# The order of products inside the feed-forward units whose weights are the stationary operand

## The chip, the cores and the metric

The kernel runs on one core of a Trainium2 chip. The metric is the device time of one execution in microseconds (us); lower is better. All inputs and the output are float32, with a batch of one and 256 positions.

## The reference, cut to what matters

Two transformer blocks follow one another. The parts that the change touches are their two feed-forward layers:

```
# first block: D_MODEL = 1024, D_FF = 4096
u = rms_norm(h, g_mlp)
h = h + jnp.square(jax.nn.relu(u @ w_ff1)) @ w_ff2
...
# second block: D_FF_2 = 2816
h2 = _rmsnorm(x, norm2_w) * (1.0 + scale2) + shift2
ffn = jnp.dot(jax.nn.silu(jnp.dot(h2, w_ffn_gate)) * jnp.dot(h2, w_ffn_up), w_ffn_down)
x = x + gate2 * ffn
```

## The kernel before, in words

Every weight matrix is read once, in units of 128 partitions by two contraction tiles by 512 columns (`raw`). ScalarE rounds a unit to its upper half (`w_hi`), VectorE subtracts to get its lower half (`w_lo`), both in a ring of four slots (`SPLIT`). The activations are kept the same way, upper and lower half side by side (`xT`, `sT`: contraction tile, half, 256 positions). A product in full precision is the sum of three: upper by upper, lower by upper, upper by lower.

Two kinds of unit matter here.

- In most units the activations are the stationary operand and 512 columns of weights move past them: `unit_pair`, `unit_rows` and `unit_wide`, all through `mm3` (L1709 to L1711), three products of 512 columns into one bank.
- In the feed-forward layers the hidden units are wanted transposed, so the weights are the stationary operand. `unit_T2` does this. A unit has four column tiles (i = 0 to 3), and each has its own PSUM bank `B[:, i, :]`. For each tile, two products of 512 columns (L1772, one for each contraction tile kk: `w_hi` by both halves of the activations side by side) and then two of 256 columns (L1775: `w_lo` by the upper half, added to the second half of the same bank). That makes 16 products a unit.

Four such units make the hidden units of a chunk, and are followed by `unit_wide` units, which multiply the previous chunk's hidden units with the second matrix: four of them in the first block (`hidden_chunk`, called for seven chunks), two in the second (`two_chunks`, ten chunks). Only these two functions call `unit_T2`.

What orders the work around it: before a unit, TensorE waits for `lo_done` (the unit's lower half is there). In the first unit of a chunk it also waits ahead of tile 0 and ahead of tile 2 for a count of `relu` or `ffn_sums`: the earlier content of banks 0 and 1, then of banks 2 and 3, has been read out. In the last unit, the last product of tile 1 adds to `first_bank`, upon which ScalarE copies from banks 0 and 1 (`hidden_minor` L743, `ffn_minor`, its copy at L962); the last product of every unit adds to `units_used`, upon which ScalarE may fill the slot anew (L787 in the first block's loop, L982 in the second's).

`unit_T2_banks` (L1787, L1790; the first block's input projection) and the 256-column products of `unit_T` (L1757 to L1759) are like it in kind and aren't changed. `unit_pair_lows_last` (L1734, L1743, L1746) takes two units near the start of the kernel: 512-column products whose bank alternates from each product to the next.

Of the kernel before, what the change touches and what calls it, by code (L numbers as in the profile page):

```python
# [7 lines left out]
P = 128  # L8
# [7 lines left out]
SEQ = 256  # L16
# [155 lines left out]
def build(nc, x, p, g_mix, w_in, b_forget, swa_sinks, w_br_swa, w_br_fox, w_mix_out, g_mlp, w_ff1, w_ff2,  # L172
# [87 lines left out]
    with ExitStack() as ctx:  # L260
        def sb(name, shape, dt=F32):
            return ctx.enter_context(nc.sbuf_tensor(name, shape, dt))
# [3 lines left out]
        def sem(name):  # L266
            return sems[name]
# [3 lines left out]
        w_hi = sb("w_hi", [P, SPLIT, 2, 512], F32R)  # L271
        w_lo = sb("w_lo", [P, SPLIT, 2, 512], F32R)
# [127 lines left out]
        B = ctx.enter_context(nc.psum_tensor("B", [P, 8, 512], F32))  # L400
# [1305 lines left out]
        def _(pe):  # L1706
            def mm3(bank, xh, xl, wh, wl, start, stop):

                nc.tensor.matmul(bank, xh, wh, start=start, stop=False)  # L1709
                nc.tensor.matmul(bank, xh, wl, start=False, stop=False)  # L1710
                return nc.tensor.matmul(bank, xl, wh, start=False, stop=stop)  # L1711
# [12 lines left out]
            def rows_of(t):  # L1724

                return slice(t * P, (t + 1) * P)
# [37 lines left out]
            def unit_T2(u, x2, kt0, first, last, sums=None, free=None):  # L1764

                s = u % SPLIT
                for i in range(4):
                    if free is not None and i % 2 == 0:
                        pe.wait_ge(sem(sums), free + i // 2)
                    cols = slice(i * P, (i + 1) * P)  # L1770
                    for kk in range(2):
                        nc.tensor.matmul(B[:, i, :], w_hi[:, s, kk, cols], x2[:, kt0 + kk, :, :].rearrange("p e n -> p (e n)"),  # L1772
                                         start=first and kk == 0, stop=False)
                    for kk in range(2):
                        m = nc.tensor.matmul(B[:, i, SEQ:2 * SEQ], w_lo[:, s, kk, cols], x2[:, kt0 + kk, 0, :], start=False,  # L1775
                                             stop=last and kk == 1)
                    if last and i == 1:
                        m.then_inc(sem("first_bank"), 1)
                m.then_inc(units_used, 1)

# [13 lines left out]
            def unit_rows(u, xh, xl, kt0, t, bank, first, last):  # L1794

                s, n = u % SPLIT, spans(u)
                rows = slice(t * P, (t + 1) * P)
                for kk in range(2):
                    m = mm3(B[:, bank, 0:n], xh[:, kt0 + kk, rows], xl[:, kt0 + kk, rows], w_hi[:, s, kk, 0:n], w_lo[:, s, kk, 0:n],
                            first and kk == 0, last and kk == 1)  # L1800
                return m
# [99 lines left out]
            for c in range(5):  # L1901
                banks = (2 * (c % 2), 2 * (c % 2) + 1)
                for kp in range(4):
# [12 lines left out]
                    if u == 1:  # L1916
                        for kk, (upper_half, lower_half) in enumerate(((sem("second_hi"), sem("second_lo")), (hi_done, lo_done))):
# [8 lines left out]
                            for t in range(TILES):  # L1926
                                m = nc.tensor.matmul(B[:, banks[t], :], xT_hi[:, 2 + kk, rows_of(t)], w_lo[:, 1, kk, :], start=False, stop=False)
# [9 lines left out]
                    else:  # L1937
                        for kk, (x_upper, upper_half, x_lower, lower_half) in enumerate((
# [9 lines left out]
                            for t in range(TILES):  # L1948
                                m = nc.tensor.matmul(B[:, banks[t], :], xT_hi[:, kk, rows_of(t)], w_lo[:, 0, kk, :], start=False, stop=False)
# [7 lines left out]
                    if u == 6:  # L1957

                        pe.wait_ge(sem("root_id"), 2)
                        for t in range(TILES):  # L1960
                            m = nc.tensor.matmul(B[:, 6, t * P:(t + 1) * P], ones, rstd_id[:, t, :], start=True, stop=True)
# [13 lines left out]
            for n in range(2 * HEADS + 4):  # L1975
# [10 lines left out]
                else:  # L1986
                    i = n - 16
# [78 lines left out]
            def hidden_chunk(j, opens):  # L2066

                for r in range(4):
                    pe.wait_ge(lo_done, j * 8 + (U_FFL + r - 7))
                    unit_T2(U_FFL + r, sT, 2 * r, r == 0, r == 3, "relu", j * 2 - 1 if r == 0 else None)  # L2070
                for r in range(4):
                    if r % 2 == 0:
                        pe.wait_ge(sem("hid_lo"), j * 2 - (1 if r == 0 else 0))
                    pe.wait_ge(lo_done, j * 8 + (U_FFL + r - 3))
                    unit_wide(U_FFL + 4 + r, xT_hi, xT_lo, r, acc, opens and r == 0, False)
# [35 lines left out]
            for kp in range(4):  # L2111
                pe.wait_ge(lo_done, U_PG + 4 + kp + 1)
                m = unit_rows(U_PG + 4 + kp, sT_hi, sT_lo, 2 * kp, 0, 6, kp == 0, kp == 3)
# [34 lines left out]
            for q in range(4, 60):  # L2148
# [20 lines left out]
                if 13 <= q < 21 and (q - 13) % 2 == 0:  # L2169
                    i = q - 13  # L2170
# [6 lines left out]
                if 33 <= q < 41 and (q - 33) % 2 == 0:  # L2177
                    n = q - 17
# [13 lines left out]
                if q >= 44 and (q - 44) % 3 == 0 and (q - 44) // 3 < R_HEADS:  # L2192
                    i = (q - 44) // 3
# [7 lines left out]
                if q >= 46 and (q - 46) % 3 == 0 and (q - 46) // 3 < R_HEADS:  # L2201
                    i = (q - 46) // 3
# [40 lines left out]
            for t in range(TILES):  # L2243
                for i, (half, kp) in enumerate(SQUARE[4:8], 4):
# [9 lines left out]
                    m = unit_rows(u, sT_hi, sT_lo, 2 * kp, t, 4 + 2 * half + t, False, kp == 3)  # L2254
# [22 lines left out]
            def two_chunks(i, opens, last=False):  # L2277

                for half in range(2):
                    for e in range(6):  # L2280
                        u = U_FNL + 6 * half + e
                        if e == 4:
                            pe.wait_ge(sem("ffn_lo"), i * 2 + (half + 1))
                        pe.wait_ge(lo_done, i * 12 + (u + 1))
                        if e < 4:
                            unit_T2(u, xT, 2 * e, e == 0, e == 3, "ffn_sums", i * 4 + (2 * half + 1) if e == 0 else None)
                        else:
                            unit_wide(u, sT_hi, sT_lo, 2 * half + e - 4, acc, opens and half == 0 and e == 4, False,
                                      7 if last and half and e == 5 else None)
# [8 lines left out]
            for t in range(TILES):  # L2298
                rows = slice(t * P, (t + 1) * P)
                for half in range(2):  # L2300
                    own = t == 1 and half == 1
                    for piece in range(2 if own else 1):
                        n = SEQ if own else 2 * SEQ
                        cols = slice(SEQ * piece, SEQ * piece + n)
                        for e in range(2):
                            k = (U_FNE + e) % SPLIT
                            o = B[:, piece if own else acc[t][half], 0:n]
                            if t == 0 and half == 0 and e == 1:
# [4 lines left out]
                                m = nc.tensor.matmul(o, sT_hi[:, e, rows], w_lo[:, k, half, cols], start=False, stop=True)  # L2313
                                continue
                            m = mm3(o, sT_hi[:, e, rows], sT_lo[:, e, rows], w_hi[:, k, half, cols],
                                    w_lo[:, k, half, cols], own and e == 0, e == 1)
# [28 lines left out]
```

## Time and profile before

| what | value |
|---|---|
| median of 3 runs | 824.3 us (824.13 to 824.35) |
| the profiled execution's own time | 823.81 us |
| its span, first to last instruction | 822.1 us |
| mean granted TensorE clock | 0.998 |
| TensorE matmul busy | 812.8 us (99%) |
| weight loads busy | 677.7 us (82%) |
| VectorE, ScalarE, GpSimd busy | 629.3, 462.9, 61.9 us |

Matmuls are pipelined and the end of one in the trace is modelled, so the duration of a product overlaps the next one's. What a product costs is read from the distance of its start to the next product's start. In the timeline, products of one line that follow each other are merged into one row with their count. "PEld" is the weight load ahead of each product; each of the products has its own.

### The profile page before, as it was taken

The page shows a single profiled execution, that of the slowest core. Times are in us where ns is not written, and L with a number is a line of the kernel's source. Part 1 is how long each engine was busy: PE and PEld are TensorE (multiplying, and loading weights), DVE is VectorE, ACT ScalarE, POOL GpSimd, SP SyncE. Part 2 cuts the span into 40 slices and gives each one's busy share as a digit, 9 for nine tenths or more (in the row PEclk, how much of TensorE's full clock was granted, in tenths as well). Part 3 has the DMA queues.
Part 4 walks back from the last instruction along what each step waited for, and adds up shares of the span by engine and source line. Part 5 has one row for each costly group of instructions (what it writes and reads, how often), then busy time and mean ns, then how long its engine had stood idle before and what let it go on. Part 6 is the DMA issues. An engine that isn't in the chain of part 4 may idle for free.

```text
span 822.1 us, 12294 instructions
## 1 busy us (share of the span) xinstructions
PE 812.8 (99%) x4272; PEld 677.7 (82%) x4272; DVE 629.3 (77%) x965; ACT 462.9 (56%) x751; POOL 61.9 (8%) x89
## 2 busy tenths in 40 slices
PE   9999999999999999999999999999999999999996
PEld 7897777898888888877978877888888888888885
DVE  5567777687888898878878997456796877677776
ACT  6657765466555555568544466446346654455444
POOL 2100000110011110301510000010000000000000
PEclk9999999999999999999999999999999999999999
DMA  9867435779999999543965574555544666655641
GB/s 302 275 198 237 136 126 182 251 273 405 346 335 340 319 323 336 191 120 106 272 213 143 164 218 137 171 154 153 180 154 128 201 189 209 196 178 172 209 130 52
DMA packets 89213, 173.15 MB, mean 211 GB/s; under 512 B 6553, under 2 KB 37001, under 8 KB 89041
## 3 DMA queue, kind: packets, MB, share of 16 engines
q1 hardware_dynamic: 83008, 142.56, 54.2%
q0 software_dynamic: 6000, 29.93, 10.5%
q8 instruction: 27, 0.44, 0.2%
q14 instruction: 18, 0.14, 0.0%
q10 hardware_dynamic: 160, 0.07, 0.0%
HBM read 170.42 MB, written 1.06 MB: 209 GB/s over the span
## 4 chain that ended last, share of the span: by engine, by line
PE 95%; DVE 2%; issue 1%; ACT 1%; POOLq 0%; POOL 0%; ACTq 0%; DVEq 0%
PE B L1709 19%; PE B L1711 19%; PE B L1710 19%; PE B L1772 15%; PE B L1775 8%; PE B L1852 2%; PE B L1787 2%; PE B L1882 2%; PE B L1860 1%; PE B L1873 1%; PE B L2126 1%; PE B L1790 1%; DVE w_lo L1032 1%; PE B L1818 0%; PE B L1809 0%
## 5 line engine op out<-in xcount | busy, mean ns | idle before, releaser
L1032 DVE TENSOR_TENSOR w_lo<-raw,w_hi 128x1024 fp32r<-128x1024 f32 (+3 forms) x154 | 184.8, 1209 | 49.4 <-ACT w_hi L569 47.9
L1709 PE MATMUL B<-w_hi,xT 128*128 128x512 f32 (+3 forms) x536 | 209.5, 391 | 0.0
L569 ACT ACTIVATE w_hi<-raw 128x1024 fp32r<-128x1024 f32 (+3 forms) x154 | 157.5, 1030 | 88.6 <-PE B L1711 74.6
L1711 PE MATMUL B<-w_hi,xT 128*128 128x512 f32 (+3 forms) x536 | 204.5, 381 | 0.0
L1710 PE MATMUL B<-w_lo,xT 128*128 128x512 f32 (+3 forms) x536 | 204.1, 381 | 0.0
L1709 PEld LDWEIGHTS B<-w_hi,xT 128*128 128x128 f32 x536 | 100.8, 188 | 20.7 <-issue 2.2
L1711 PEld LDWEIGHTS B<-w_hi,xT 128*128 128x128 f32 x536 | 100.7, 188 | 19.8
L1710 PEld LDWEIGHTS B<-w_lo,xT 128*128 128x128 f32 x536 | 100.9, 188 | 17.4
L1772 PE MATMUL B<-xT,w_hi 128*128 128x512 f32 x320 | 100.5, 395 | 0.0
L982 ACT ACTIVATE w_hi<-raw 128x1024 fp32r<-128x1024 f32 x60 | 62.2, 1055 | 42.5 <-PE B L1775 30.9
L1302 DVE TENSOR_TENSOR w_lo<-raw,w_hi 128x1024 fp32r<-128x1024 f32 x56 | 67.2, 1221 | 21.7 <-ACT w_hi L787 20.8
L1709 PE MATMUL B<-w_hi,sT 128*128 128x512 f32 (+1 forms) x201 | 78.9, 393 | 0.0
L1638 DVE TENSOR_TENSOR w_lo<-raw,w_hi 128x1024 fp32r<-128x1024 f32 x60 | 72.5, 1220 | 7.6 <-ACT w_hi L982 7.6
L1710 PE MATMUL B<-w_lo,sT 128*128 128x512 f32 (+1 forms) x201 | 77.9, 388 | 0.0
L1711 PE MATMUL B<-w_hi,sT 128*128 128x512 f32 (+1 forms) x201 | 77.9, 387 | 0.0
L787 ACT ACTIVATE w_hi<-raw 128x1024 fp32r<-128x1024 f32 x56 | 57.5, 1053 | 35.0 <-PE B L1775 30.6
L1775 PEld LDWEIGHTS B<-xT,w_lo 128*128 128x128 f32 x320 | 60.1, 188 | 14.1
L1772 PE MATMUL B<-sT,w_hi 128*128 128x512 f32 x224 | 70.3, 395 | 0.0
L1775 PE MATMUL B<-xT,w_lo 128*128 128x256 f32 x320 | 62.9, 278 | 0.0
L1310 DVE SCALAR_TENSOR_TENSOR Z<-Z,small 128x1536 f32<-128x1536 f32 x28 | 50.8, 1813 | 0.0
L1775 PEld LDWEIGHTS B<-sT,w_lo 128*128 128x128 f32 x224 | 42.1, 188 | 9.9
L1772 PEld LDWEIGHTS B<-xT,w_hi 128*128 128x128 f32 x320 | 49.4, 189 | 0.9 <-DVE Z L1624 0.2
(270 smaller groups left out, 1071.4 us busy)
## 6 DMA issues: line engine op xcount, KB each, us to landing
raw<-in_w_in_dram SPq DMA_DIRECT2D x79, 512.0 KB, 3.9
raw<-in_w_ff_dram SPq DMA_DIRECT2D x64, 512.0 KB, 7.4
Z<-in_w_ada_dram POOLq DMA_DIRECT2D x32, 768.0 KB, 7.6
raw<-in_w_ffn_gate_dram SPq DMA_DIRECT2D x44, 256.0 KB, 3.4
raw<-in_w_ffn_up_dram SPq DMA_DIRECT2D x44, 256.0 KB, 4.1
raw<-in_w_ffn_down_dram SPq DMA_DIRECT2D x20, 512.0 KB, 4.3
raw<-in_w_mix_out_dram SPq DMA_DIRECT2D x8, 512.0 KB, 3.7
raw<-in_w_ple_gate_dram SPq DMA_DIRECT2D x8, 512.0 KB, 4.3
```

Of the source, the lines that this page charges most:

```text
L569: nc.scalar.activation(w_hi[:, u % SPLIT, :, 0:n], raw[:, st.slot[u], :, 0:n], ACT.Copy).then_inc(hi_done, 1)
L787: nc.scalar.activation(w_hi[:, u % SPLIT, :, :], raw[:, st.slot[u], :, :], ACT.Copy).then_inc(hi_done, 1)
L982: nc.scalar.activation(w_hi[:, u % SPLIT, :, :], raw[:, st.slot[u], :, :], ACT.Copy).then_inc(hi_done, 1)
L1032: nc.vector.tensor_tensor(w_lo[:, u % SPLIT, :, 0:n], raw[:, st.slot[u], :, 0:n], w_hi[:, u % SPLIT, :, 0:n].bitcast(F32), ALU.subtract).t ...
L1302: nc.vector.tensor_tensor(w_lo[:, u % SPLIT, :, :], raw[:, st.slot[u], :, :], w_hi[:, u % SPLIT, :, :].bitcast(F32), ALU.subtract).then_in ...
L1310: nc.vector.scalar_tensor_tensor(ada_acc[:, 1536 * q:1536 * (q + 1)], ada_raw[:, q, :], silu_now, ada_acc[:, 1536 * q:1536 * (q + 1)], ALU ...
L1638: nc.vector.tensor_tensor(w_lo[:, u % SPLIT, :, :], raw[:, st.slot[u], :, :], w_hi[:, u % SPLIT, :, :].bitcast(F32), ALU.subtract).then_in ...
L1709: nc.tensor.matmul(bank, xh, wh, start=start, stop=False)
L1710: nc.tensor.matmul(bank, xh, wl, start=False, stop=False)
L1711: return nc.tensor.matmul(bank, xl, wh, start=False, stop=stop)
L1772: nc.tensor.matmul(B[:, i, :], w_hi[:, s, kk, cols], x2[:, kt0 + kk, :, :].rearrange("p e n -> p (e n)"), start=first and kk == 0, stop=False)
L1775: m = nc.tensor.matmul(B[:, i, SEQ:2 * SEQ], w_lo[:, s, kk, cols], x2[:, kt0 + kk, 0, :], start=False, stop=last and kk == 1)
```

## The change

In `unit_T2` the column tiles are taken in pairs (b = 0: tiles 0 and 1, b = 1: tiles 2 and 3). For a pair, the four 512-column products come first: contraction tile 0 for both tiles, then contraction tile 1 for both; so the bank alternates from product to product, and two products in a row have the same moving operand. Then come the pair's four 256-column products in the same order. The products themselves, their number, the waits ahead of tiles 0 and 2 and the increments behind tile 1 and behind the unit are those of before.

```diff
             def unit_T2(u, x2, kt0, first, last, sums=None, free=None):
 
                 s = u % SPLIT
-                for i in range(4):
-                    if free is not None and i % 2 == 0:
-                        pe.wait_ge(sem(sums), free + i // 2)
-                    cols = slice(i * P, (i + 1) * P)
+                for b in range(2):
+                    if free is not None:
+                        pe.wait_ge(sem(sums), free + b)
                     for kk in range(2):
-                        nc.tensor.matmul(B[:, i, :], w_hi[:, s, kk, cols], x2[:, kt0 + kk, :, :].rearrange("p e n -> p (e n)"),
-                                         start=first and kk == 0, stop=False)
+                        for i in (2 * b, 2 * b + 1):
+                            nc.tensor.matmul(B[:, i, :], w_hi[:, s, kk, i * P:(i + 1) * P], x2[:, kt0 + kk, :, :].rearrange("p e n -> p (e n)"),
+                                             start=first and kk == 0, stop=False)
                     for kk in range(2):
-                        m = nc.tensor.matmul(B[:, i, SEQ:2 * SEQ], w_lo[:, s, kk, cols], x2[:, kt0 + kk, 0, :], start=False,
-                                             stop=last and kk == 1)
-                    if last and i == 1:
+                        for i in (2 * b, 2 * b + 1):
+                            m = nc.tensor.matmul(B[:, i, SEQ:2 * SEQ], w_lo[:, s, kk, i * P:(i + 1) * P], x2[:, kt0 + kk, 0, :], start=False,
+                                                 stop=last and kk == 1)
+                    if last and b == 0:
                         m.then_inc(sem("first_bank"), 1)
                 m.then_inc(units_used, 1)
```

## Rows read from the trace of the kernel before

**Rows 1.** The page: the span, the engines' busy time, the chain by engine.

```profile
span 822.1 us, 12294 instructions
...
PE 812.8 (99%) x4272; PEld 677.7 (82%) x4272; DVE 629.3 (77%) x965; ACT 462.9 (56%) x751; POOL 61.9 (8%) x89
...
PE 95%; DVE 2%; issue 1%; ACT 1%; POOLq 0%; POOL 0%; ACTq 0%; DVEq 0%
```

**Rows 2.** Waits of TensorE, longest in total (the only row).

```profile
PE B L1890 <- DVE ones_r L1130: 1.4, 1, 1.4
```

**Rows 3.** Groups by line and shape on TensorE: unit_T2's products.

```profile
L1772 PE MATMUL B<-xT,w_hi 128*128 128x512 f32 x320 | 100.5, 395 | 0.0
...
L1772 PE MATMUL B<-sT,w_hi 128*128 128x512 f32 x224 | 70.3, 395 | 0.0
L1775 PE MATMUL B<-xT,w_lo 128*128 128x256 f32 x320 | 62.9, 278 | 0.0
L1775 PE MATMUL B<-sT,w_lo 128*128 128x256 f32 x224 | 44.0, 278 | 0.0
```

**Rows 4.** Line L1775: who waited for it (us in total, times).

```profile
  ACT Z L962: 35.9, 19
  ACT w_hi L982: 30.9, 18
```

**Rows 5.** Timeline of TensorE in a unit_T2 stretch: start, duration in us.

```profile
303.19 0.63 PE L1772 MATMUL B<-sT,w_hi 128*128 128x512 f32 x2
303.65 0.39 PE L1775 MATMUL B<-sT,w_lo 128*128 128x256 f32 x2
303.88 0.62 PE L1772 MATMUL B<-sT,w_hi 128*128 128x512 f32 x2
304.35 0.40 PE L1775 MATMUL B<-sT,w_lo 128*128 128x256 f32 x2
304.58 0.63 PE L1772 MATMUL B<-sT,w_hi 128*128 128x512 f32 x2
```

**Rows 6.** Timeline: the first product of one unit_T2 stretch, and the first behind it.

```profile
316.17 0.39 PE L1772 MATMUL B<-sT,w_hi 128*128 128x512 f32 x1
...
327.30 0.40 PE L1709 MATMUL B<-w_hi,xT 128*128 128x512 f32 x1
```

**Rows 7.** Timeline of the second unit in unit_pair_lows_last.

```profile
16.24 1.07 PE L1734 MATMUL B<-w_hi,xT 128*128 128x512 f32 x4
17.15 1.07 PE L1746 MATMUL B<-w_lo,xT 128*128 128x512 f32 x4
18.05 1.07 PE L1743 MATMUL B<-w_hi,xT 128*128 128x512 f32 x4
```

**Rows 8.** Timeline where 256-column products (unit_T) follow products of 512 columns.

```profile
171.61 0.28 PE L1757 MATMUL B<-sT,w_hi 128*128 128x256 f32 x1
171.72 0.28 PE L1758 MATMUL B<-sT,w_hi 128*128 128x256 f32 x1
...
172.08 0.28 PE L1758 MATMUL B<-sT,w_hi 128*128 128x256 f32 x1
...
172.68 0.28 PE L1757 MATMUL B<-sT,w_hi 128*128 128x256 f32 x1
```

**Rows 9.** Timeline where products of 512 columns follow a run of 256-column ones.

```profile
399.50 0.40 PE L1709 MATMUL B<-w_hi,xT 128*128 128x512 f32 x1
...
400.43 0.39 PE L1710 MATMUL B<-w_lo,xT 128*128 128x512 f32 x1
400.66 0.39 PE L1711 MATMUL B<-w_hi,xT 128*128 128x512 f32 x1
400.89 0.39 PE L1709 MATMUL B<-w_hi,xT 128*128 128x512 f32 x1
```

**Rows 10.** Windows: busy time by engine, then PEclk, the granted clock.

```profile
15.90:18.80 2.90, 2.90 (x15) 2.39 (x14) 2.06 (x4) 2.87 (x7) 0.00 (x0) 1.00 1.10 352
...
316.10:327.40 11.30, 11.30 (x67) 9.85 (x66) 10.79 (x11) 5.38 (x6) 0.53 (x1) 1.00 0.95 318
```

**Rows 11.** Timeline of TensorE's first products of the kernel.

```profile
1.44 2.93 PE L1890 MATMUL B<-ones_r 128*128 128x512 f32 x6 [1.44 <-DVE ones_r L1130]
...
5.37 1.20 PE L1890 MATMUL B<-ones_r 128*128 128x512 f32 x2
```

## The prediction

> **What bounds the kernel now.** I read the page first. TensorE is busy 99% of the span and holds 95% of the chain that ended last [rows 1]; the other engines are well below. Then its waits: in the whole span TensorE waits once for another engine, 1.4 us at the very start [rows 2]. So the kernel lasts as long as its 4272 products take one behind another, and an edit that moves nothing but the order of products can only work through their spacing. The groups by line say how many are touched: 320 + 224 of 512 columns at L1772 and as many of 256 columns at L1775 [rows 3], 1088 in all, or 68 units, or 136 pairs of column tiles. The durations there (395 and 278 ns) overlap and are no price. The price is in the timeline: two column tiles, 303.19 to 304.58, take 1.39 us [rows 5]. A whole stretch of four units, eight pairs, takes 327.30 - 316.17 = 11.13 us [rows 6], 1.391 us for a pair, and the stretches that I compared are alike. All 136 pairs are 189 us, 23% of the span.
>
> **What the change removes and adds: nothing but an order.** A pair has four products of 512 columns and four of 256 before and after, each with its own weight load. The waits for the banks stand ahead of the first and the ninth product of a unit in both versions. `first_bank` comes with the eighth product and `units_used` with the sixteenth in both. That matters because ScalarE is queued behind these two: it waits 35.9 us in all for the copies at L962 and 30.9 us for the slots at L982 [rows 4]. Since the counts of products ahead of each signal are the same, ScalarE, VectorE behind it, and the DMAs that refill the raw slots see each signal earlier or later only by what the pairs themselves gain or lose; I cost them at nothing. Their cover is that TensorE doesn't wait on them now [rows 2]; with a pair some ns longer they have more room. Were pairs shorter, the most they could be late is the gain itself.
>
> **The price of four 512-column products in a row.** Within the present pattern the two starting at 303.19 take 0.46 us and the two at 303.88 take 0.47 us, so about 0.233 us each [rows 5]. Two other places give bounds. (a) `unit_pair_lows_last` is the nearest form: runs of four, the bank alternating with each product, the same moving operand twice in succession, as after the change. Its first two runs of four take 17.15 - 16.24 = 0.91 and 18.05 - 17.15 = 0.90 us, 0.227 a product [rows 7]. But these are in the middle of an all-512 stretch. So neither an alternating bank nor a repeated moving operand costs or saves anything by itself. (b) Behind a run of 256-column products, the first four of 512 columns take 400.43 - 399.50 = 0.93 us, and only then does a product come to 0.23 and less [rows 9]. After the change, every run of four follows 256-column products, so (b) is the nearer case. I take 0.93, with 0.91 and 0.94 (four times 0.235, a little over the present pattern) as ends.
>
> **The price of four 256-column products in a row.** In the present pattern two take 0.23 us: 303.88 - 303.65 and 304.58 - 304.35 [rows 5], about 0.116 each. In `unit_T`, the first one behind products of 512 columns takes 0.11 us, and the first four 172.08 - 171.61 = 0.47 us; the nine shown take 172.68 - 171.61 = 1.07 us, so a later one costs 0.12 [rows 8]. The short price of 0.11 is thus had only directly behind the long products; today each pair of tiles gets it twice, after the change once. I take 0.47, with 0.46 (four at today's 0.116) and 0.48 (four at 0.12) as ends.
>
> **The sum.** A pair after the change: 0.93 + 0.47 = 1.40 us, against 1.391, so +0.009 us. Times 136 pairs: +1.2 us. The rows are rounded to 0.01 us, and 0.01 us a pair is 1.4 us, so the sign is weak. Order inside the `unit_wide` behind each of 17 stretches might shift by some 0.01 us, 0.2 us in all, which I leave out. Against the profiled execution that is 823.81 + 1.2 = 825.0; it stands 0.5 us below the median of the runs, so against the median the forecast is 824.3 + 1.2 = 825.5 us, +0.15%.
>
> A measurement of this kernel can tell about 0.2%, 1.65 us, from no change; that is 0.012 us a pair.
>
> **A rule of the Trainium skill beside it.** Rows say that the spacing of one kind of product depends on what stands ahead of it (0.93 against 0.91 us for four of 512 columns, 0.11 against 0.12 for one of 256) [rows 7, 8, 9]. The Trainium skill, page "TensorE: Matmul & The Clock Gate", section "Back-to-back issue gap", gives the isolated gap at the high clock as the columns over 2.4 plus 2.5 ns, that is 216 and 109 ns, and a lower figure for streams with weight loads, 131 ns at 512 columns. The trace doesn't agree with either: 227 and 120 ns in long runs. By that rule order doesn't enter and the change would be worth exactly nothing: 824.3 us.
>
> **The rivals.**
>
> *The short switches go, and nothing else (0.20).* Long runs stand at 0.227 and 0.12 us a product. If the present pattern's surplus over these is a cost of each switch between 512 and 256 columns, the pair loses half its switches: 4 x 0.2267 + 4 x 0.12 = 1.387 us is the floor, 4 ns below 1.391; with half the surplus left 1.389. That is -0.3 to -0.6 us: 823.9 us, no measurable change. For it: 512-column products do settle at 0.227 [rows 7]. Against it: they need more than four products to settle behind short ones [rows 9].
>
> *Faster (0.06).* The four long products settle at once (0.907, as in rows 7) and the four short ones keep the price of rows 8 (0.47): 1.377 us, -0.014 a pair, -1.9 us: 822.4 us. It counts as faster only if both hold. Against it: the short 0.11 looks like a lead that is given back in the next long products, whose first four take 0.93; both at once would take the lead and not return it.
>
> *Slower: every run stays unsettled (0.12).* Four of 512 columns at 0.235 and four of 256 at 0.12, as if the weight load ahead of each short product set its pace: 0.94 + 0.48 = 1.42 us, +0.029 a pair, +3.9 us: 828.2 us. It decides from +0.012 a pair on. For it: runs of 256 columns stand at 0.12 [rows 8] although two in a row have 0.116 now, and the first product behind a run of short ones is as long as 0.235. Against it: by the fourth long product the spacing has fallen to 0.23 [rows 9].
>
> *The granted clock falls (0.02).* Granted clock is 1.00 in the present stretches and also where banks alternate with each product [rows 10], and TensorE has no gap that the new order would open. Products of 512 columns did stand 2.93 / 6 = 0.49 us apart at the kernel's start, 2.15 times as far [rows 11]; if one stretch of 11.13 us ran so, it would cost 12.8 us: 837 us. The Trainium skill, same page, section "A second HAM failure mode: psum-queue depth-cycling", tells of a kernel with 512-column products that cycled through banks each iteration, idled briefly between groups and so had its clock swing; that speaks against this change, and the alternating unit at 16.24 us does not show it.
>
> **How the numbers follow.** The forecast has 0.60, with its own range 1.395 to 1.405 us a pair, +0.5 to +1.9 us: 824.8 to 826.2 us. A little of it, 0.04, lies above the 0.2% bound. Within 0.2%: 0.56 + 0.20 = 0.76. Slower: 0.04 + 0.12 + 0.02 = 0.18. Faster: 0.06. For 8 in 10 the range takes the forecast and the settled case and stops short of the outer two: from 823.5 (the floor of 1.387, less a little for the runs' spread) to 827.0 us (1.411 a pair, between the forecast's end and the unsettled case).
>
> **What the changed profile would show.** The timeline's merged rows hold four products each, L1772 and L1775 in turn. Right: such a period lasts 1.40 us, a stretch of four units 11.2 us, the four long ones 0.93 and the four short ones 0.47; PEclk stays 1.00; the waits of TensorE stay at one row; the ScalarE waits behind the last short product are as long as before within a few us. The settled rival shows 11.10 to 11.12 us a stretch, the faster one 11.02, the unsettled one 11.36. What would make the prediction wrong: a spacing inside runs of four that no place in this trace has, above all of 256-column products that alternate between two banks, the one form that it doesn't show; or new rows in TensorE's waits at the bank waits.

## The result, and the profile after

The changed kernel takes 825.45 us (median of 22 runs, 825.11 to 827.31), the kernel before 824.12 us in 22 runs of the same comparison; the ratio is 1.0018, 95% interval 1.0012 to 1.0024. That is 1.3 us by the medians and 1.5 us by the ratio: a real but very small loss. The ratio lies just inside the 0.2% that the prediction set as its bound; the upper end of the interval, 0.24%, lies outside it. The forecast was 825.5 us.

The page of the changed kernel: span, busy time, chain by engine [against rows 1].

```profile
span 823.5 us, 12294 instructions
...
PE 814.2 (99%) x4272; PEld 679.1 (82%) x4272; DVE 629.4 (76%) x965; ACT 462.8 (56%) x751; POOL 61.8 (8%) x89
...
PE 98%; issue 0%; DVE 0%; ACT 0%; POOLq 0%; POOL 0%; ACTq 0%; DVEq 0%
```

The same 4272 products, and 1.4 us more of TensorE busy for 1.4 us more of span; VectorE, ScalarE and GpSimd have the busy times that they had, within 0.1 us. TensorE's waits, whole list [against rows 2]:

```profile
PE B L1891 <- DVE ones_r L1130: 1.4, 1, 1.4
PE B L1944 <- ACT w_hi L643: 0.2, 1, 0.2
```

The second wait is one at the kernel's start, in code that the change doesn't touch; some of the experiments below have it and some don't. No wait has come in the feed-forward layers. But the list leaves one out in both kernels. The first stretch of the second block is longer than the others, 11.453 against 11.137 us before and 11.500 against 11.200 after, because TensorE stands ahead of tile 2 until VectorE has read out the banks. The products' modelled ends cover this gap; the rows of the weight loads show it, before and after:

```profile
644.27 0.30 PEld L1772 LDWEIGHTS B<-xT,w_hi 128*128 128x128 f32 x2 [0.22 <-DVE Z L1624]
...
644.80 0.30 PEld L1772 LDWEIGHTS B<-xT,w_hi 128*128 128x128 f32 x2 [0.22 <-DVE Z L1624]
```

So the prediction's "TensorE waits once" [rows 2] is one wait short, and this wait matters in the runs of eight and sixteen below. It is as long after the change as before. So the loss is in the spacing of products. Timeline of TensorE: start, duration, count, at the end of one stretch of `unit_T2`, and the first products behind it [against rows 5, 9].

```profile
302.91 1.09 PE L1772 MATMUL B<-sT,w_hi 128*128 128x512 f32 x4
303.84 0.64 PE L1776 MATMUL B<-sT,w_lo 128*128 128x256 f32 x4
304.31 1.09 PE L1772 MATMUL B<-sT,w_hi 128*128 128x512 f32 x4
305.24 0.63 PE L1776 MATMUL B<-sT,w_lo 128*128 128x256 f32 x4
305.71 0.40 PE L1709 MATMUL B<-w_hi,xT 128*128 128x512 f32 x1
...
316.64 0.61 PE L1772 MATMUL B<-sT,w_hi 128*128 128x512 f32 x2
...
327.84 0.40 PE L1709 MATMUL B<-w_hi,xT 128*128 128x512 f32 x1
```

Four products of 512 columns take 303.84 - 302.91 = 0.93 us and four of 256 take 304.31 - 303.84 = 0.47 us; the pair 1.40. In single starts, a pair in the middle of a stretch has 932 ns for its long products and 461 for its short ones before, and 929 and 474 after (the mean of a unit's two pairs): the loss is in the short ones. The whole stretch takes 327.84 - 316.64 = 11.20 us against 11.13 [rows 6]. Windows of the changed kernel, with the granted clock behind POOL's column [against rows 10]:

```profile
316.10:327.40 11.30, 11.30 (x65) 9.79 (x64) 10.69 (x11) 5.37 (x6) 0.74 (x2) 1.00 0.90 314
```

The clock stays at 1.00.

The starts in the trace, taken to the nanosecond, make the account of the span's 1.4 us (1.47 unrounded). All 17 stretches of `unit_T2` sum to 190.73 us against 189.65, +1.08. The `unit_wide` units behind fifteen of them (those followed by another stretch) sum to 114.90 against 114.43, +0.48: a run of 48 products took 305.71 to 316.64 = 10.93 us above, and 10.89 before, as these rows of the kernel before show.

```profile
305.28 0.40 PE L1709 MATMUL B<-w_hi,xT 128*128 128x512 f32 x1
...
316.17 0.39 PE L1772 MATMUL B<-sT,w_hi 128*128 128x512 f32 x1
```

The units behind the first stretch of each block took the same as before; those behind each of the other thirteen took 0.037 us more. The units behind the two stretches left out of the fifteen add 0.07 us. Everything else is 0.16 us shorter, 0.1 of it ahead of the first stretch; two executions of one kernel differ by more.

### The profile page after: what moved, and what is told of

It reads as the page before. It is cut to its first block, busy times and chain, and to the rows that moved or that the text cites. A ratio compares the mean times of both kernels' runs of the same rounds, so it can differ in the third digit from the quotient of the medians.

```text
span 823.5 us, 12294 instructions
## 1 busy us (share of the span) xinstructions
PE 814.2 (99%) x4272; PEld 679.1 (82%) x4272; DVE 629.4 (76%) x965; ACT 462.8 (56%) x751; POOL 61.8 (8%) x89
## 4 chain that ended last, share of the span: by engine, by line
PE 98%; issue 0%; DVE 0%; ACT 0%; POOLq 0%; POOL 0%; ACTq 0%; DVEq 0%
PE B L1709 20%; PE B L1711 20%; PE B L1710 20%; PE B L1772 15%; PE B L1776 8%; PE B L1853 2%; PE B L1788 2%; PE B L1883 2%; PE B L1861 1%; PE B L1874 1%; PE B L2127 1%; PE B L1791 1%; PE B L1819 0%; PE B L1810 0%; PE B L1821 0%; PE B L1759 0%
## 5 line engine op out<-in xcount | busy, mean ns | idle before, releaser
L1772 PE MATMUL B<-xT,w_hi 128*128 128x512 f32 x320 | 87.2, 394 | 0.0
L982 ACT ACTIVATE w_hi<-raw 128x1024 fp32r<-128x1024 f32 x60 | 62.2, 1054 | 43.1 <-PE B L1776 31.1
L787 ACT ACTIVATE w_hi<-raw 128x1024 fp32r<-128x1024 f32 x56 | 57.5, 1053 | 35.7 <-PE B L1776 30.9
L1772 PEld LDWEIGHTS B<-xT,w_hi 128*128 128x128 f32 x320 | 55.3, 189 | 8.1 <-DVE Z L1624 0.2
L1772 PE MATMUL B<-sT,w_hi 128*128 128x512 f32 x224 | 61.0, 394 | 0.0
L1776 PEld LDWEIGHTS B<-xT,w_lo 128*128 128x128 f32 x320 | 49.1, 189 | 6.8
L1776 PE MATMUL B<-xT,w_lo 128*128 128x256 f32 x320 | 50.9, 281 | 0.0
L1709 PEld LDWEIGHTS B<-w_hi,sT 128*128 128x128 f32 x201 | 37.8, 188 | 8.2 <-issue 1.0
```

The costliest lines, as they stand in the source:

```text
L787: nc.scalar.activation(w_hi[:, u % SPLIT, :, :], raw[:, st.slot[u], :, :], ACT.Copy).then_inc(hi_done, 1)
L982: nc.scalar.activation(w_hi[:, u % SPLIT, :, :], raw[:, st.slot[u], :, :], ACT.Copy).then_inc(hi_done, 1)
L1772: nc.tensor.matmul(B[:, i, :], w_hi[:, s, kk, i * P:(i + 1) * P], x2[:, kt0 + kk, :, :].rearrange("p e n -> p (e n)"), start=first and kk ...
L1776: m = nc.tensor.matmul(B[:, i, SEQ:2 * SEQ], w_lo[:, s, kk, i * P:(i + 1) * P], x2[:, kt0 + kk, 0, :], start=False, stop=last and kk == 1)
```

## The experiments

Each is described by how it differs from the changed kernel; of long lines and unchanged parts the diffs show only what matters, and "..." stands for the rest. A "long" product has 512 moving columns, a "short" one 256. "Stretch" is the time from the first product of four `unit_T2` units to the first product behind them, for all stretches but the first of each block; these agree within 2 ns. The first unit of a stretch stands behind `unit_wide` products and is shorter than those behind it (2.780 against 2.807 us in the changed kernel, 2.777 against 2.787 before), so a middle unit is compared with a middle unit.

### Four and four, bank kept

```diff
-                    for kk in range(2):
-                        for i in (2 * b, 2 * b + 1):
+                    for i in (2 * b, 2 * b + 1):
+                        for kk in range(2):
                             nc.tensor.matmul(B[:, i, :], w_hi[:, s, kk, i * P:(i + 1) * P], ...
-                    for kk in range(2):
-                        for i in (2 * b, 2 * b + 1):
+                    for i in (2 * b, 2 * b + 1):
+                        for kk in range(2):
                             m = nc.tensor.matmul(B[:, i, SEQ:2 * SEQ], w_lo[:, s, kk, i * P:(i + 1) * P], ...
```

> Four products of 512 columns and then four of 256, as in the changed kernel, but each tile's two products stand together, so that the bank alternates once in four products and no moving operand is repeated. Theory of run length (a product's spacing depends only on the kind and number of products just ahead of it): nothing differs, a pair stays at 1.400 us, the stretch of four units at 11.20 us, the run at +1.3 to +1.5 us against the kernel before. Rival, bank and operand order: the alternation of banks or the repeated moving operand costs the 8 ns a pair, so the pair goes back to 1.392 us and the run to +0 us.

825.72 us, ratio to the kernel before 1.002 (1.0011 to 1.003). Timeline of TensorE:

```profile
303.25 1.09 PE L1772 MATMUL B<-sT,w_hi 128*128 128x512 f32 x4
304.18 0.64 PE L1776 MATMUL B<-sT,w_lo 128*128 128x256 f32 x4
304.65 1.09 PE L1772 MATMUL B<-sT,w_hi 128*128 128x512 f32 x4
```

304.65 - 303.25 = 1.40 us a pair, stretch 11.20: the changed kernel's numbers without its alternating banks.

### Two and two, bank alternating

```diff
                     for kk in range(2):
                         for i in (2 * b, 2 * b + 1):
                             nc.tensor.matmul(B[:, i, :], w_hi[:, s, kk, i * P:(i + 1) * P], ...
-                    for kk in range(2):
                         for i in (2 * b, 2 * b + 1):
                             m = nc.tensor.matmul(B[:, i, SEQ:2 * SEQ], w_lo[:, s, kk, i * P:(i + 1) * P], ...
```

> Runs of two and two as in the kernel before, but the bank alternates with every product and the moving operand is repeated. Run length: as the kernel before, 1.392 us a pair, stretch 11.14 us, +0 us. Bank and operand order: as the changed kernel, 1.400 us a pair, stretch 11.20 us, +1.3 us.

823.94 us, ratio 0.9999 (0.9989 to 1.0009). Timeline of TensorE:

```profile
303.37 0.63 PE L1772 MATMUL B<-sT,w_hi 128*128 128x512 f32 x2
303.84 0.39 PE L1775 MATMUL B<-sT,w_lo 128*128 128x256 f32 x2
304.07 0.63 PE L1772 MATMUL B<-sT,w_hi 128*128 128x512 f32 x2
304.53 0.40 PE L1775 MATMUL B<-sT,w_lo 128*128 128x256 f32 x2
304.76 0.63 PE L1772 MATMUL B<-sT,w_hi 128*128 128x512 f32 x2
```

304.76 - 303.37 = 1.39 us a pair, stretch 11.14. With the run before it, this settles the place of the loss: not the alternation of banks and not the repeated moving operand, but the length of the runs.

### Runs of eight

```diff
                             nc.tensor.matmul(B[:, i, :], w_hi[:, s, kk, i * P:(i + 1) * P], ...
+                for b in range(2):
                     for kk in range(2):
                         for i in (2 * b, 2 * b + 1):
                             m = nc.tensor.matmul(B[:, i, SEQ:2 * SEQ], w_lo[:, s, kk, i * P:(i + 1) * P], ...
```

> Eight products of 512 columns over four banks, then eight of 256; the signal first_bank comes four short products later. Run length with settling (the long ones come down to 0.227 us after about five, the short ones stay at 0.120 us): the long ones 234+235+229+232+231+227+227+227 = 1842 ns, the short ones 0.117 and seven times 0.120 = 957 ns, so 2.80 us a unit, the same as the changed kernel (two pairs of 1.400), +1.0 to +1.5 us against the kernel before. Rival, no settling (the surplus grows with the length of the runs, 5 ns a pair at two and 13 at four over 1.387): 2.83 us a unit, 11.3 us a stretch, +3.3 us or more.

824.96 us, ratio 1.0011 (1.0002 to 1.0021). Timeline of TensorE, a unit in the middle of a stretch:

```profile
297.43 2.00 PE L1772 MATMUL B<-sT,w_hi 128*128 128x512 f32 x8
299.27 1.12 PE L1777 MATMUL B<-sT,w_lo 128*128 128x256 f32 x8
300.22 2.00 PE L1772 MATMUL B<-sT,w_hi 128*128 128x512 f32 x8
```

A unit takes 2.79 us. The eight long ones take 1.84 us as settling has it. The short ones take 0.95, 119 ns each, a little less than expected (the first one 113 ns and not 117), so a unit is 2.793 and not 2.799 us. The rival (2.83) falls. The stretch takes 11.146 us, 9 ns more than in the kernel before. About half of what makes this run slower is something else, a row in TensorE's waits:

```profile
PE B L1772 <- DVE Z L1624: 0.5, 1, 0.5
```

Here the wait for banks 2 and 3 stands ahead of the fifth product and not the ninth, and the first stretch of the second block takes 11.934 us against 11.453 before: 0.48 of the 0.94 us by which all stretches and the units behind them are longer.

### Runs of one

```diff
-                    for kk in range(2):
-                        for i in (2 * b, 2 * b + 1):
+                    for i in (2 * b, 2 * b + 1):
+                        for kk in range(2):
                             nc.tensor.matmul(B[:, i, :], w_hi[:, s, kk, i * P:(i + 1) * P], ...
-                    for kk in range(2):
-                        for i in (2 * b, 2 * b + 1):
                             m = nc.tensor.matmul(B[:, i, SEQ:2 * SEQ], w_lo[:, s, kk, i * P:(i + 1) * P], ...
```

> One product of 512 columns and one of 256 in turn. Run length: every short product stands directly behind a long one and has the low price, 113 to 116 ns, every long one stands behind one short one and has 231 to 234 ns: 4 x (232.5 + 114.5) = 1.388 us a pair, stretch 11.10 us, -0.5 us against the kernel before; if the long ones come near 0.227 us as well, 1.365 us a pair and -3.6 us. Rival, a fixed cost of each switch of kind: more switches make it longer than the kernel before, over 1.392 us a pair and over 0 us.

827.23 us, ratio 1.0038 (1.0023 to 1.0052): the slowest order. Timeline of TensorE:

```profile
301.51 0.40 PE L1772 MATMUL B<-sT,w_hi 128*128 128x512 f32 x1
301.75 0.28 PE L1774 MATMUL B<-sT,w_lo 128*128 128x256 f32 x1
301.87 0.40 PE L1772 MATMUL B<-sT,w_hi 128*128 128x512 f32 x1
302.11 0.28 PE L1774 MATMUL B<-sT,w_lo 128*128 128x256 f32 x1
302.22 0.40 PE L1772 MATMUL B<-sT,w_hi 128*128 128x512 f32 x1
...
302.93 0.40 PE L1772 MATMUL B<-sT,w_hi 128*128 128x512 f32 x1
```

Eight products last 302.93 - 301.51 = 1.42 here and 11.29 / 8 = 1.411 us over the stretch. The short ones are 0.11 to 0.12, but a long one behind a single short one takes up to 0.24 us. My reading of "what stands just ahead" missed this: I expected 1.388. A fixed cost of each switch has the right sign here, but not elsewhere. Over the floor of 4 x 226.7 + 4 x 120 = 1386.7 ns a pair, the surplus is 25 ns with runs of one, 5 with two, 13 with four, 6.5 with eight. A stretch has 31, 15, 7 and 3 returns from short to long inside it, so that its surplus over 11.093 us is 6, 3, 15 and 18 ns for one return; in the middle units it is 7, 3, 17 and 20. Neither theory gives all four.

### Halved weight loads of the short products, two orders

```diff
+n_lo = P if last else P // 2
-... matmul(B[:, i, SEQ:2 * SEQ], w_lo[:, s, kk, i * P:(i + 1) * P], ...
+... matmul(B[0:n_lo, i, SEQ:2 * SEQ], w_lo[:, s, kk, i * P:i * P + n_lo], ...
```

> The changed kernel's order, but in the first three units of each stretch a 256-column product loads only 64 of its 128 stationary columns (it leaves out half of the lower-half products there; the last unit of each stretch is whole). Theory, the weight load sets the pace of the short ones: they fall from 0.118-0.120 us to about 0.110, and a pair from 1.400 us to 1.36-1.38 us in those units, the kernel by 51 units x 2 pairs x 0.02 to 0.04 = 2 to 4 us. Rival, the pace doesn't come from the load's length: a pair stays at 1.400 us and the kernel at +1.3 us against the kernel before.

> The same cut of the weight loads in the order of the kernel before, two and two. Theory, the load sets the pace and the long products pay for it: a pair falls from 1.392 us by 0.01 us or more, towards the same value as in the order of four and four, so that the two orders no longer differ. Rival: a pair stays at 1.392 us, and the two orders differ by 8 ns as before.

The diff is that of the first run; the second one has, besides, the order of the kernel before, two and two. A product with 64 stationary columns also writes 64 partitions of its bank in place of 128, which the runs do not separate from the shorter load.

Four and four: 823.58 us once, beside 823.94 for the kernel before. Two and two: 826.03 us once. Timelines of TensorE, four and four, then two and two:

```profile
295.94 1.08 PE L1773 MATMUL B<-sT,w_hi 128*128 128x512 f32 x4
296.87 0.62 PE L1777 MATMUL B<-sT,w_lo 128*64 128x256 f32 x4
...
298.72 1.08 PE L1773 MATMUL B<-sT,w_hi 128*128 128x512 f32 x4
```

```profile
296.01 0.63 PE L1773 MATMUL B<-sT,w_hi 128*128 128x512 f32 x2
...
298.83 0.63 PE L1773 MATMUL B<-sT,w_hi 128*128 128x512 f32 x2
```

With four and four, two pairs take 298.72 - 295.94 = 2.78 us, 2.773 to the nanosecond where a middle unit took 2.807: 1.387 a pair, which is the floor, so the surplus is gone. The short ones fell to some 116 ns and not to the expected 110. With two and two, a pair takes (298.83 - 296.01) / 2 = 1.41 us, 1.407 in single starts against 1.393: less work and 14 ns more a pair than with full loads. So the number of stationary columns of the short products takes part in the surplus, but loading fewer of them can be slower as well as faster, and the theory that both orders would meet falls.

### Fewer moving columns in the short products

```diff
+n_lo = SEQ if last else 192
-... B[:, i, SEQ:2 * SEQ] ... x2[:, kt0 + kk, 0, :]
+... B[:, i, SEQ:SEQ + n_lo] ... x2[:, kt0 + kk, 0, 0:n_lo]
```

> The changed kernel's order; in the first three units of each stretch a short product moves 192 columns in place of 256 and so leaves out a quarter of the lower-half products there. Theory, the pace of short products in a run of four is set by the load of their 128 stationary columns: nothing gets faster, the short ones stay at 0.118 to 0.120 us and a unit at 2.80 us. Rival, the moving columns set it: 64 columns at the spacing that 512 columns have (0.227 us / 512 = 0.44 ns a column) are 28 ns a product, 0.23 us less a unit, 2.57 us, and the kernel by 51 x 0.23 = 11 us or so faster.

821.78 us once, beside 824.02 for the kernel before. Timeline of TensorE:

```profile
294.87 1.10 PE L1773 MATMUL B<-sT,w_hi 128*128 128x512 f32 x4
295.82 0.58 PE L1777 MATMUL B<-sT,w_lo 128*128 128x192 f32 x4
...
297.61 1.10 PE L1773 MATMUL B<-sT,w_hi 128*128 128x512 f32 x4
```

Two pairs take 297.61 - 294.87 = 2.74 us, a middle unit 2.734 in place of 2.807: 36 ns a pair for 256 moving columns fewer, where the moving columns alone would have given 113. So neither side is right: about a third of what the columns would give came back. In single starts the four short ones stand 86, 113, 113 and 112 ns apart, and the long ones behind them 252, 233, 231 and 226. Only the first short one gets the full gain of its fewer columns (86 ns, where one of full width behind settled long products has the 113 of [rows 8]), the other three stop at 113, and the first long one gives 17 ns back against the 235 of the full width. That is the "lead that is given back" of the prediction, seen enlarged.

### Halved weight loads of the long products

```diff
+n_hi = P if first or last else P // 2
-... matmul(B[:, i, :], w_hi[:, s, kk, i * P:(i + 1) * P], ...
+... matmul(B[0:n_hi, i, :], w_hi[:, s, kk, i * P:i * P + n_hi], ...
```

> The changed kernel's order; in the second and third unit of each stretch the 512-column products load 64 of their 128 stationary columns (half of the upper-half products left out there), the short ones load all 128. If the surplus of long products behind short ones (0.233 against 0.227 us) is paid for their own loads, a unit falls from 2.80 to 2.77 us as it did with halved loads of the short ones. If it is paid for the loads of the short ones, a unit stays at 2.80 us.

825.16 us once. Timeline of TensorE, two pairs of one of these units:

```profile
297.52 1.08 PE L1773 MATMUL B<-sT,w_hi 128*64 128x512 f32 x4
298.44 0.64 PE L1777 MATMUL B<-sT,w_lo 128*128 128x256 f32 x4
298.93 1.08 PE L1773 MATMUL B<-sT,w_hi 128*64 128x512 f32 x4
299.85 0.64 PE L1777 MATMUL B<-sT,w_lo 128*128 128x256 f32 x4
300.33 1.08 PE L1773 MATMUL B<-sT,w_hi 128*64 128x512 f32 x4
```

300.33 - 297.52 = 2.81, to the nanosecond 2.801 us a unit against 2.807 for a middle unit of the changed kernel: 5 ns less a unit, where the same halving of the short ones gave 33. The long ones take 0.92 in place of 0.93, but the short ones take 0.48 to 0.49 in place of 0.47. So in this order the surplus hangs mainly on the stationary columns of the short products and little on those of the long ones.

### The units behind a stretch

```diff
+                if last:
+                    for b in range(2):
...
+                        for i in (2 * b, 2 * b + 1):
+                            for kk in range(2):
+                                nc.tensor.matmul(B[:, i, :], w_hi[:, s, kk, i * P:(i + 1) * P], ...
+                            for kk in range(2):
+                                m = nc.tensor.matmul(B[:, i, SEQ:2 * SEQ], w_lo[:, s, kk, i * P:(i + 1) * P], ...
+                else:
...
```

> The changed order in the first three units of a stretch, the order of before in the last unit. It tests the term that the prediction left out, the unit_wide units behind a stretch: they took 10.890 us (first block) and 5.450 us (second) before, 10.927 and 5.487 after the change. If they depend only on the last few products ahead of them, they go back to 10.890 or 10.908 and 5.450 or 5.468, and the stretch to 3 x 2.800 + 2.784 = 11.18 us. Rival, they depend on something further back: 10.927 and 5.487 stay.

824.83 us once, beside 823.94 for the kernel before. Timeline of TensorE, the last unit of a stretch and the first product behind it:

```profile
302.76 0.63 PE L1773 MATMUL B<-sT,w_hi 128*128 128x512 f32 x2
...
305.56 0.40 PE L1709 MATMUL B<-w_hi,xT 128*128 128x512 f32 x1
```

The `unit_wide` units behind take 10.907 and 5.467 us: half of the 37 ns come back, the second of the two values that the theory left open. The stretch misses: it takes 11.193 us and not 11.18, and the last unit itself still takes 2.799 us, not 2.784. So what stood sixteen products ahead of those units, in the third unit of the stretch, still counts a little.

### Runs of sixteen

```diff
+                for kind in (("upper", "lower") if kt0 % 4 == 0 else ("lower", "upper")):
+                    for b in range(2):
+                        if free is not None and kind == "upper":
+                            pe.wait_ge(sem(sums), free + b)
+                        for kk in range(2):
+                            for i in (2 * b, 2 * b + 1):
+                                if kind == "upper":
+                                    m = nc.tensor.matmul(B[:, i, :], w_hi[:, s, kk, i * P:(i + 1) * P], ...
+                                else:
+                                    m = nc.tensor.matmul(B[:, i, SEQ:2 * SEQ], w_lo[:, s, kk, i * P:(i + 1) * P], ...
+                        if last and kind == "upper" and b == 0:
+                            m.then_inc(sem("first_bank"), 1)
```

> Units alternate between eight long ones first and eight short ones first, so a stretch is 8 long, 16 short, 16 long, 16 short, 8 long: two changes from short to long instead of 8 (changed kernel) and 16 (before), and the unit_wide behind it follows long products. Theory from the runs of four and eight (each return to long products costs 13 ns over 4 x 0.2267 + 4 x 0.12 a pair, whatever the run's length from four on): 8 x 1.3867 + 2 x 0.013 = 11.12 us a stretch against 11.14 before and 11.20 after the change, the unit_wide units at 10.890 and 5.450: -0.3 to -0.4 us against the kernel before, within the noise of a time but plain in the trace. Rival, the surplus keeps growing with the runs: above 11.14 us.

824.31 us, ratio 1.0004 (0.9995 to 1.0013). Timeline of TensorE: the end of a stretch with its last long products and the start of the next; then the first stretch of the second block.

```profile
301.76 2.08 PE L1777 MATMUL B<-sT,w_lo 128*128 128x256 f32 x16
303.67 2.00 PE L1774 MATMUL B<-sT,w_hi 128*128 128x512 f32 x8
305.51 0.39 PE L1709 MATMUL B<-w_hi,xT 128*128 128x512 f32 x1
...
316.39 1.98 PE L1774 MATMUL B<-sT,w_hi 128*128 128x512 f32 x8
...
642.88 1.09 PE L1774 MATMUL B<-xT,w_hi 128*128 128x512 f32 x4
644.46 1.20 PE L1774 MATMUL B<-xT,w_hi 128*128 128x512 f32 x4 [0.48 <-DVE Z L1624]
```

The stretch takes 11.133 us and not the expected 11.12: with two returns over a floor of 11.093, 20 ns a return. The expectation's 13 had counted four returns in a stretch of eights, which has three inside it; a middle unit of eights also has 20 ns for its one return. Single starts show what they consist of, in both runs: behind short products the first five long ones stand 234, 236, 228, 232 and 231 ns apart (28 ns over the settled 227), and behind settled long ones the first two short ones 113 and 119 (8 ns under the settled 120). The units behind take 316.39 - 305.51 = 10.88 us, the floor of 48 x 226.7 ns. Both are better than in the kernel before (11.137 and 10.890). But the time isn't, because of the last two rows: the second four long products need banks 2 and 3, which VectorE has not read out (`Z L1624`), and TensorE stands from 643.81 (four products of 0.23 from 642.88) to 644.46. The short products that used to stand ahead of this wait no longer cover it.

### Runs of sixteen, but for the first stretches

With the new argument true (`opens` in the first block, `opens and half == 0` in the second), `unit_T2` uses the order of the kernel before; else the runs of sixteen.

```diff
-                                    unit_T2(U_FFL + r, sT, 2 * r, r == 0, r == 3, "relu", j * 2 - 1 if r == 0 else None)
+                                    unit_T2(U_FFL + r, sT, 2 * r, r == 0, r == 3, "relu", j * 2 - 1 if r == 0 else None, opens)
```

> Runs of sixteen, but the first stretch of each block in the order of the kernel before. In the runs of sixteen these two stretches took 11.20 and 11.92 us in place of 11.15 and 11.45, since the long products of the second pair of banks come four short products earlier and TensorE then waited there for the banks (0.88 us between two products). Theory: the two go back to 11.15 and 11.45, the other fifteen stay at 11.133, the unit_wide behind those at 10.880 and 5.440 us: 0.2 to 0.3 us less than the kernel before in the trace, no measurable change in time. Rival, the wait comes from elsewhere: 11.92 stays.

823.63 us, ratio 0.9998 (0.9989 to 1.0007). Timeline of TensorE in the same place:

```profile
643.67 0.62 PE L1773 MATMUL B<-xT,w_hi 128*128 128x512 f32 x2
644.14 0.40 PE L1776 MATMUL B<-xT,w_lo 128*128 128x256 f32 x2
644.55 0.72 PE L1773 MATMUL B<-xT,w_hi 128*128 128x512 f32 x2
```

Now the wait falls between 644.14 and 644.55, and the stretch takes 11.458 us in place of 11.921: the cause of that loss is shown. Over all 17 stretches and the units behind, this order is 0.21 us shorter than the kernel before by the starts in the trace. In the measured time it can't be told from it.

## Why the prediction was right

**What bounds the kernel: right.** TensorE's busy time and the span grew by the same 1.4 us. No wait came in the feed-forward layers, and ScalarE and VectorE changed nothing: ScalarE's waits for the last short product are 36.3, 31.1 and 30.9 us (L962, L982, L787) against 35.9, 30.9 and 30.6.

**Signals and waits cost nothing: right** for this change, since their places in the order were kept. The runs of eight and of sixteen show the price where they aren't: 0.48 and 0.46 us at one bank wait.

**Four long products 0.93 us, four short ones 0.47: right as sums.** The choice of the rows behind a run of short products, over those of the settled run (0.91), decided the sign. The sum of +9 ns a pair, 1.2 us in all, measured +8 ns a pair: the stretch at 11.200 against 11.137 us, and +1.08 us over 136 pairs. One reason given for it was not: the low price of 0.11 us was to be had once in each run of short products. In a middle unit no short product has it (they stand 116 to 120 ns apart). Only the first unit of a stretch does, where the first short one, behind settled long products, has 113 ns.

**The term left out: off by more than its size.** For the `unit_wide` units behind a stretch I put at most 0.01 us, 0.2 us in all. They took 0.037 us more behind every stretch but the first of each block, 0.55 us in all. The place named there was right. A run of long products behind runs of four short ones keeps paying longer than the four products that I priced: nine of them stand more or less far apart (224 to 236 ns) before they settle at 227.

**How much of the hit was luck.** The forecast of 825.5 us lies 0.05 us from the median, closer than its parts were known. It was made of one term a little too large (1.2 for 1.08), one left out (0.55), and 0.16 us that went the other way elsewhere. And its rows were rounded to 0.01 us, which alone is 1.4 us in 136 pairs, as the prediction says. That the sign was right rests on the choice of rows; that the size was right to a tenth is luck.

**The rivals.** The settled case (1.387 to 1.389 a pair) and the unsettled one (1.42) did not come. Banks and moving operand cost nothing, as the unit at 16.24 us had said [rows 7]; two runs show it from both sides.

The clock did not fall: PEclk is 1.00 in the changed stretches. The price of that rival was read wrongly from [rows 11], though. The 2.93 us is a modelled duration that holds more than the spacing. In single starts four of those products stand 427 ns apart, 1.88 times the settled 227, which would make 9.8 us of one stretch and not 12.8. Nor does a row tie that spacing to the granted clock: the trace's record of the clock begins 6.4 us into the span, behind these products. The Trainium skill, page "TensorE: Matmul & The Clock Gate", section "A second HAM failure mode: psum-queue depth-cycling", tells of a kernel that cycled through the banks and idled briefly between groups of products. TensorE's waits here show no such idle times. Banks that alternate on every product, without such gaps, leave PEclk at 1.00.

The Trainium skill, same page, section "Back-to-back issue gap", gives the spacing by the number of columns; by that, order would not count. The runs contradict it: four orders of the same 64 products take 11.14, 11.15, 11.20 and 11.29 us a stretch.

**What stays open** is why. Shown is that the surplus over the settled spacing depends on the run lengths (25, 5, 13, 6.5 ns a pair for one, two, four, eight). For the two longest orders, eight and sixteen, one number fits: 20 ns for each return to long products. In shorter runs the long products don't settle before the next short ones come, and a return costs 7, 3 and 17 ns with runs of one, two and four. Shown too is that with runs of four the surplus vanishes when the short products' stationary columns are halved and falls by only 5 of 33 ns a unit when the long ones' are. The same halving of the short ones makes runs of two slower by 14 ns a pair. Whether it works through the load's length or through the fewer partitions written is not shown. A lead that is gained on the short products and given back on the long ones is visible in single starts. No rule that I tried gives all the sums: not a cost for each switch, not the load as the pace, not the settling alone.

## What to carry to other kernels

Where TensorE doesn't wait, work out the surplus of the present order over the settled spacing before writing a new one: here 5 ns in 1392, 0.7 us of 824. No order of the full products that was tried got a stretch below the settled sum. Price the new order from a place in the trace where the same kind of product stands behind the same kind of run, not from the middle of a uniform stretch. Keep each bank wait as many products from the start as it was: the products ahead of it are its cover. And look for hidden waits in the rows of the weight loads, since the modelled ends of products can cover a gap of 0.2 us.

## What the runs showed of the hardware that was not expected

- The order of the same 64 products changes their time without a simple trend in the run length: 11.29 us alternating one by one, 11.14 by twos, 11.20 by fours, 11.15 by eights, 11.13 by sixteens.
- Less work can be slower: with 64 of 128 stationary columns in the short products, runs of two went from 1.393 to 1.407 us a pair in a middle unit, runs of four from 1.403 to 1.387.
- Forty-eight products of 512 columns took 10.880, 10.890, 10.907, 10.927 or 10.944 us by what stood ahead of them (sixteens, twos, eights, fours, ones).
